# Second block of a two-block decoder: attention and output projection placed between the units of the input projection

## The chip, the cores and the metric
The kernel runs on one core of one Trainium2 chip. The metric is the device time of one execution in microseconds (us), from the first to the last instruction and what the launch puts around them. TensorE (PE) multiplies matrices into PSUM; VectorE (DVE) and ScalarE (ACT) compute on PSUM and SBUF; GpSimd (POOL) does the same slowly and issues transfers of its own; SyncE (SP) issues the loads of the weights. Each engine takes its instructions in program order, and they wait for one another through semaphores.

## The reference, cut to what matters
Two blocks of two layers each run one after the other on 256 tokens of width 1024. The change is nearly all in the second block:

```
for l in range(2):
    mod = cond @ w_mod[l] + b_mod[l]                 # six vectors of 1024
    h = rms_norm(x, norm_mix) * (1 + sc_a) + sh_a
    mq, mk, mv, dq, dk, dv = split(h @ w_in)         # six times 512 columns
    # q and k: rms_norm over each head of 64 (times a weight of 64), then a rotation of the
    # first 16 elements by cos, sin of the position
    o_m = rms_norm(causal_attention(mq, mk, mv))     # 8 heads of 64
    o_d = rms_norm((softmax(s1) - lam * softmax(s2)) @ dv) * (1 - lam_init)   # 4 heads, v of 128
    x = x + g_a * (concat(o_m, o_d) @ w_out)
    h = rms_norm(x, norm_ffn) * (1 + sc_f) + sh_f
    x = x + g_f * ((silu(h @ w_gate) * (h @ w_up)) @ w_down)
```

With 256 tokens and a block of 256, the "moba" attention is a plain causal one.

## The kernel before
All weights come through a ring of six slots of 1 MB each (`ring`), filled by SP in the order in which PE uses them. A layer of the second block has these parts, one after the other:

- **Modulation.** POOL has formed `w_mod * cond` for this layer beforehand (`modulation(l)`, 24 pieces of 1 MB, into `pmod`). PE sums it over partitions (L1385, L1390).
- **Input projection.** Twelve units of 256 columns (L882, 32 matmul records each), into four PSUM banks in turn. After each of the eight units of q and k, ACT squares (L802), DVE sums per head (L1929), ACT takes the root with `Sqrt` (L804), DVE takes the reciprocal (L1932), scales (L1935), multiplies by the norm's weight (L1937) and rotates (twelve instructions of 128x32, L1943 to L1948). PE transposes the result (L1143) behind the next unit, and ACT copies it to `qT` (L807). The four units of v are only copied (L797).
- A barrier of all engines.
- **Attention** in eight units: four pairs of moba heads, four diff heads. For each, PE forms scores (L1053), DVE scales and masks (L1570) and takes row maxima (L1574, L1579), ACT takes four exponentials with row sums (L616), DVE divides (L1587 to L1597), PE transposes the probabilities (L1094), ACT copies them (L631), PE multiplies with v (L1114), and DVE copies the result to `om` (L1609). At the end the outputs are squared, summed, rooted (L813) and scaled on DVE and ACT, in two halves (L1614 to L1630).
- A barrier, 16 transposes of `om` (L849), four copies (L818), and the **output projection** (L1033, 64 records, first all of token tile 0, then all of tile 1).
- **Residual and norm**: DVE multiplies by the gate and adds (L1956, L1958), ACT sums squares (L768) and takes a root (L771), DVE scales (L1881), PE transposes (L849), DVE modulates (L1890). Then the gated feed-forward (L875, L893).

For layer 1, POOL's `modulation(1)` starts after layer 0's second barrier of the second block, that is, after the attention:

```
                if b == 2 * BARRIERS_1 + 1:
                    modulation(1)
```

The tables of the rotation are computed by DVE and ACT (`Sin`) at the start of the second block.

Of the kernel before, what the change touches and what calls it, by code (L numbers as in the profile page):

```python
# [14 lines left out]
P = 128  # L15
D = 1024
# [36 lines left out]
          ("gate_b", 32), ("norm_mix", 8), ("norm_ffn", 8), ("b_mod", 48)]  # L53
N_PAR = sum(n for _, n in PARAMS)
N_PARAM_LOADS = DEPTH * (len(PARAMS) + 5) + 4
GAINS = [("moba_q", 64), ("moba_k", 64), ("diff_q", 64), ("diff_k", 64), ("moba_out", 64), ("diff_sub", 128),
         ("lambda", 256)]
# [57 lines left out]
def build(nc, a, out, known):  # L115
    with ExitStack() as ctx:
# [31 lines left out]
        small = sb("small", [P, 256])  # L148
        ARENA = 27700
# [5 lines left out]
        def view(*shape, parts=P, at=None):  # L155
# [7 lines left out]
            names = "abcd"[:len(shape)]  # L163
# [82 lines left out]
        top[0] = 3000  # L246
        gains = view(sum(n for _, n in GAINS))
        grow = view(2, D)
        modT, Amod = view(32), view(2, KT)
        cosb, sinb = view(NT, ROPE_HALF), view(NT, ROPE_HALF)  # L250
        ang = view(4, NT * ROPE_HALF)
        vtm, om = view(NT, D), view(NT, D)
        tok_scaled = vtm
        qT = view(16, SEQ)
        ys_tmp = view(NT, D, at=top[0])
        tq, tsq = view(2, 512), view(2, 512)
        rope = view(6, NT * 4 * ROPE_HALF)
        angi = ang[:, 3, :].bitcast(I32)
        Sm2, PT2 = view(4, 2, PACK), view(2, 2, PACK)
# [4 lines left out]
        ys_tmp = tok_scaled  # L264
        oT8 = oT[:, 0:8, :]

        def units_of(seg):
            return UNITS1 if seg == "b1" else UNITS2

        def o_bank(seg, i):  # L270
            return 6 if seg == "b1" else 6 + i % 2
# [12 lines left out]
        goff = {}  # L284
        o = 0
        for name, n in GAINS:
            goff[name] = (o, n)
            o += n

        def prm(l, name, i=0, n=1):  # L290
            return par[:, l, poff[name][0] + i:poff[name][0] + i + n]

        def gain(name):
            return gains[:, goff[name][0]:goff[name][0] + goff[name][1]]
# [11 lines left out]
        def unit_list(segment):  # L306
# [21 lines left out]
            elif kind == "in2":  # L328
                w = kview(a["w_in_2"][l])
                for i in range(12):  # L330
                    yield ("in2", l, i), [(0, 256, w[:, :, UNIT * i:UNIT * i + 256])]
# [99 lines left out]
        def _(pool):  # L431
            barrier = barrier_of(pool)

            def step(ins):
                ins.then_inc(*made("pool"))
                pool.wait_ge(S.sem("pool"), S.count["pool"])
# [74 lines left out]

            for kind in CREDITED:
                if known:
                    pool.sem_inc(S.sem(kind), known.per_turn[kind])
            for b in range(N_BARRIERS):
# [9 lines left out]
                if b == 2 * BARRIERS_1 + 1:  # L525
                    modulation(1)

        @block.scalar
        def _(act):
            barrier = barrier_of(act)  # L530

            def step(ins, *key):
                ins.then_inc(*made("act", *key))

# [66 lines left out]
            def norm_roots(*key):  # L601
                for t in range(NT):
# [3 lines left out]
            def attention(l, units, Sb, PTb, seg):  # L606
                n = len(units)
                for i in range(n + 2):
                    if i < n:
                        u, b = units[i], i % 2  # L610

                        act.wait_ge(*ready("dve", "nm", seg, l, u))
                        for qt, (k0, nk) in enumerate(KEYS):
                            for h in range(2):
                                s = Sb[:, i % 4, h, k0:k0 + nk]
                                step(act.activation(s, s, ACT.Exp, bias=nm[:, b, qt, h:h + 1],  # L616
                                                    accum_out=den[:, b, qt, h:h + 1]), "exp", seg, l, u)
                        if u[0] == "swa":
                            step(act.activation(es[:, b], es[:, b], ACT.Exp), "exp", seg, l, u)
                    if seg == "b1" and i in G[7]:  # L620
                        gates(l, 1, (7,))
                    if i >= 2:
                        turned(units[i - 2], l, seg, i - 2, PTb)

            def turned(v, l, seg, i, PTb):

                act.wait_ge(*ready("pe_job", "pt", seg, l, v))
# [1387 lines left out]
```

## Time and profile before

| what | value |
|---|---|
| median of 3 runs | 2629.13 us (2629.05 to 2632.51) |
| span of the profiled execution | 2622.4 us |
| what lies around the span, against the median | 6.7 us |
| PE busy | 2340.6 us, 89% of the span |
| layer 1, second block, input projection | 2197.8 to 2287.2 |
| layer 1, attention up to the second barrier | 2287.2 to 2339.7 |
| layer 1, turning `om`, output projection | to 2373.8 |

The profiled execution has no time of its own beside its span; the span stands 6.7 us under the median of the other runs. The granted clock of PE is given in the windows as a share of full speed (1.00 is 2.4 GHz, 0.50 is 1.2 GHz).

### The profile page before, as it was taken

The numbers are of one execution on the slowest core, as the hardware profiler recorded it, in microseconds if no ns is written. First come the engines' busy times: TensorE is split into PE (matmuls) and PEld (weight loads), VectorE is DVE, ScalarE is ACT, GpSimd is POOL, SyncE is SP. The second block draws the span as 40 slices with busy tenths as digits, with TensorE's granted clock in tenths as the row PEclk, the third lists the DMA queues.
The fourth block names the chain that finished last, engine by engine and source line by source line (L and its number), as shares of the span: only waits on it lengthen the run. The fifth ranks groups of instructions, "written<-read, shape, count | busy, mean of one in ns | idle before, by whom it ended". The sixth has DMA issues, their size and how long they took to land.

```text
span 2622.4 us, 29759 instructions
## 1 busy us (share of the span) xinstructions
PE 2340.6 (89%) x12542; PEld 1827.3 (70%) x12542; DVE 700.0 (27%) x1477; ACT 334.9 (13%) x756; POOL 451.1 (17%) x328
## 2 busy tenths in 40 slices
PE   8997788999899958939899999979589998968998
PEld 7786565777687846637788888868457777746776
DVE  0132643000204163471211111154620104451011
ACT  0031220000002123000000000021300001230000
POOL 2000000000000000399910000000199930000000
PEclk9999789999999977969999999979689998969999
DMA  8332212444533221269978888644167744403443
GB/s 248 113 97 81 88 57 97 130 151 130 183 109 113 97 89 41 67 220 329 347 264 265 264 266 265 227 150 145 64 208 236 268 155 134 144 1 115 147 148 103
DMA packets 313420, 416.61 MB, mean 159 GB/s; under 512 B 15356, under 2 KB 272616, under 8 KB 313320
## 3 DMA queue, kind: packets, MB, share of 16 engines
q1 hardware_dynamic: 290112, 346.64, 40.5%
q0 software_dynamic: 13056, 50.33, 5.7%
q10 hardware_dynamic: 10152, 18.20, 2.0%
q8 instruction: 75, 1.23, 0.2%
q14 instruction: 25, 0.20, 0.0%
HBM read 414.10 MB, written 1.05 MB: 158 GB/s over the span
## 4 chain that ended last, share of the span: by engine, by line
PE 50%; DVE 7%; DMA 2%; ACT 1%; issue 0%; SPq 0%; DVEq 0%; ACTq 0%
PE psum L875 22%; PE psum L882 6%; PE psum L893 6%; PE psum L978 5%; PE psum L1033 3%; DMA ring<-in_exp_w 2%; PE psum L1363 1%; PE psum L938 1%; PE psum L1385 1%; PE psum L1018 1%; DVE small L1574 1%; DVE xT L1890 1%; DVE arena L1570 0%; PE psum L1390 0%; DVE arena L1514 0%
## 5 line engine op out<-in xcount | busy, mean ns | idle before, releaser
L875 PE MATMUL psum<-xT,ring 128*128 128x256 f32 (+1 forms) x3904 | 874.5, 385 | 15.0 <-DVE xT L1890 5.5
L875 PEld LDWEIGHTS psum<-xT,ring 128*128 128x128 f32 (+1 forms) x3904 | 742.4, 191 | 148.5 <-issue 23.7
L875 PEld LDWEIGHTS psum<-arena,ring 128*128 128x128 f32 x2816 | 320.0, 192 | 28.7 <-issue 23.8
L875 PE MATMUL psum<-arena,ring 128*128 128x128 f32 x2816 | 322.4, 276 | 11.0 <-DMA ring<-in_exp_w 8.8
L893 PE MATMUL psum<-ring,arena 128*128 128x512 f32 x528 | 231.5, 592 | 0.0
L882 PE MATMUL psum<-ring,xT 128*128 128x256 f32 (+3 forms) x1024 | 213.5, 368 | 6.4 <-DVE xT L1890 6.4
L882 PEld LDWEIGHTS psum<-ring,xT 128*128 128x128 f32 x1024 | 186.2, 200 | 29.1 <-DVE xT L1890 6.9
L519 POOL IOTA arena<- 128x128 int32 x1 | 0.2, 234 | 1061.4 <-DVEq L371 1061.4
L1474 DVE TENSOR_TENSOR arena<-arena,psum 128x512 f32<-128x512 f32 (+1 forms) x36 | 23.2, 643 | 594.2 <-PE psum L875 594.2
L893 PEld LDWEIGHTS psum<-ring,arena 128*128 128x128 f32 x528 | 100.4, 190 | 113.4 <-issue 111.8
L504 POOL TENSOR_TENSOR arena<-arena,cond 128x2048 f32<-128x2048 f32 x48 | 173.4, 3613 | 7.6 <-DMA arena<-in_w_mod 6.7
L978 PE MATMUL psum<-ring,arena 128*128 128x512 f32 x352 | 157.8, 593 | 1.5 <-DVE arena L1551 1.5
L491 POOL DMA_DIRECT2D arena<-in_w_mod x48 | 44.3, 923 | 583.1 <-DVEq L371 569.8
L1551 DVE TENSOR_TENSOR arena<-arena,psum 128x256 f32<-128x256 f32 (+1 forms) x48 | 19.1, 399 | 360.0 <-PE psum L875 359.6
L507 POOL TENSOR_TENSOR arena<-arena 128x1024 f32<-128x1024 f32 x48 | 113.7, 2369 | 3.8
L978 PEld LDWEIGHTS psum<-ring,arena 128*128 128x128 f32 x352 | 63.9, 191 | 66.7 <-issue 65.0
L560 ACT ACTIVATE arena<-psum 128x512 f32<-128x512 f32 (+1 forms) x36 | 20.2, 561 | 639.4 <-PE psum L875 639.4
L1094 PE MATMUL psum<-ident,arena 128*128 128x128 f32 x168 | 38.2, 385 | 46.4 <-DVE arena L1597 18.7
L1363 PE MATMUL psum<-oT,arena 128*128 128x256 f32 x320 | 71.3, 386 | 5.4 <-DMA arena<-in_w_branch 5.4
L1363 PEld LDWEIGHTS psum<-oT,arena 128*128 128x128 f32 x320 | 61.9, 194 | 14.8 <-DMA arena<-in_w_branch 6.2
L616 ACT ACTIVATE arena<-arena,small 128x256 f32<-128x256 f32 (+1 forms) x128 | 56.6, 442 | 112.0 <-DVE small L1579 111.9
L1094 PEld LDWEIGHTS psum<-ident,arena 128*128 128x128 f32 x168 | 28.0, 199 | 61.4 <-DVE arena L1597 23.8
(352 smaller groups left out, 1977.9 us busy)
## 6 DMA issues: line engine op xcount, KB each, us to landing
ring<-in_exp_w SPq DMA_DIRECT2D x120, 1024.0 KB, 7.9
ring<-in_w_in SPq DMA_DIRECT2D x80, 1024.0 KB, 5.1
arena<-in_w_mod POOLq DMA_DIRECT2D x48, 1024.0 KB, 8.3
ring<-in_ffn_w SPq DMA_DIRECT2D x30, 1024.0 KB, 5.9
ring<-in_w_gate SPq DMA_DIRECT2D x20, 1024.0 KB, 7.6
ring<-in_w_up SPq DMA_DIRECT2D x20, 1024.0 KB, 10.0
ring<-in_w_down SPq DMA_DIRECT2D x20, 1024.0 KB, 5.0
ring<-in_w_out SPq DMA_DIRECT2D x16, 1024.0 KB, 4.8
```

The source lines that it names most:

```text
L491: pool.dma_start(modw[:, j % 3, :].rearrange("p (k c) -> p k c", k=KT), w_mod[:, :, j * UNIT:(j + 1) * UNIT]).then_inc(S.sem("modw%d" % (j ...
L504: step(pool.tensor_tensor(w.rearrange("p (k c) -> p k c", k=KT), w.rearrange("p (k c) -> p k c", k=KT), cond[:].unsqueeze(2).broadcast_to( ...
L507: step(pool.tensor_tensor(w[:, 0:1024], w[:, 0:1024], w[:, 1024:2048], ALU.add))
L616: step(act.activation(s, s, ACT.Exp, bias=nm[:, b, qt, h:h + 1], accum_out=den[:, b, qt, h:h + 1]), "exp", seg, l, u)
L875: ins = pe.matmul(dst, w[:, k * 256 + c0:k * 256 + c0 + m], act_t[:, k, :], start=(k == 0), stop=(k == KT - 1))
L882: ins = pe.matmul(dst, act_t[:, k, t * P:t * P + P], w[:, k * 256 + c0:k * 256 + c0 + n], start=(k == 0), stop=(k == KT - 1))
L893: ins = pe.matmul(psum[:, 4 + 2 * t + h, :], gT[:, s % 3, f * 256 + t * P:f * 256 + t * P + P], w2[:, f * D + h * 512:f * D + h * 512 + 51 ...
L938: ins = pe.matmul(psum[:, 6 + k // 4, (k % 4) * P:(k % 4) * P + P], x[:, t, k * P:k * P + P], gather[:, t, :], start=(t == 0), stop=(t == ...
L978: ins = pe.matmul(psum[:, 4 + h, :], gT[:, s % 3, f * P:f * P + P], w2[:, f * D + h * 512:f * D + h * 512 + 512], start=(s == 0 and f == 0 ...
L1033: ins = pe.matmul(psum[:, 4 + 2 * t + h, :], src[:, k, t * P:t * P + P], ws[k2][:, i * D + h * 512:i * D + h * 512 + 512], start=(k == 0), ...
L1094: ins = pe.transpose(psum[:, 4 + h, o:o + P], Sb[:, i % 4, h, o:o + P], ident[:])
L1363: ins = pe.matmul(dst, (wb_first[:, k] if k < 5 else wb_last[:, k - 5])[:, c * P:c * P + P], oT[:, k, :], start=(k == rows_of[0]), stop=(k ...
```

## The change
The attention, the norm of its outputs and the output projection of the second block are written in one order with the twelve projection units, by hand, for PE, ACT and DVE. The two barriers are gone. In detail:

- The units come in the order `ORDER2`; the projection uses two banks instead of four.
- The head norm: the root is taken as `Exp(-0.5 * Ln(...))` on ACT instead of `Sqrt` and a reciprocal on DVE; the norm's weight is multiplied in by ACT's copy to `qT` (`keep_heads`) and, for the first 16 elements, is held in the rotation's tables (`tabA`, `tabB`), which POOL builds (`turn_tables`). The rotation takes seven instructions instead of twelve.
- The probabilities of the moba heads are not divided: the norm of the output makes up for it, with the square of the row sum times eps added to the sum of squares (`out_sums`). For the diff heads only the second half is scaled, by `lam` times the ratio of the row sums (`differ`).
- The norm of the outputs runs for each unit (`square_outs`, `out_sums`, `out_roots` with Ln and Exp, `norm_outs`, `keep_outs`), on PSUM, and each unit's output is transposed by itself (`turn_outs`).
- The output projection is cut into 16 pieces (`join(l, t, k)`), put between the last units.
- `modulation(1)` waits for the last output projection piece of layer 0. The angles and `Sin` move to before the first block's feed-forward. `norm_roots` makes a first `Sqrt` before it waits. Twelve small loads of parameters are added at the start, seven per layer leave ACT's queue, and five per layer enter POOL's.

The core of the diff (kept: what ACT does per unit, one stretch of each engine's order, and the place of `modulation(1)`):

```diff
-                        step(act.activation(tsq[:, n, :], psum[:, i % 4, :], ACT.Square), "sq", l, i)
-                        act.wait_ge(*ready("dve", "headsum", l, i))
-                        step(act.activation(rt16[:, 8 * n:8 * n + 8], ss16[:, 8 * n:8 * n + 8], ACT.Sqrt,
-                                            bias=eps[:, 2:3], scale=1.0 / HD), "headroot", l, i)
+            def head_roots(l, n):
+                i = ORDER2[n]
+                b = QK.index(i) % 2
+                act.wait_ge(*ready("dve", "headsum", l, i))
+                step(act.activation(ri8[:, b], ss8[:, b], ACT.Ln, bias=eps[:, 2:3]), "headlog", l, i)
+                act.wait_ge(*ready("act", "headlog", l, i))
+                step(act.activation(ri8[:, b], ri8[:, b], ACT.Exp, scale=-0.5), "headroot", l, i)
+            def out_roots(l, p):
+                m, d = (4, HD) if p < 4 else (2, P)
+                act.wait_ge(*ready("dve", "outsum", l, p))
+                step(act.activation(ro4[:, p % 2, 0:m], os4[:, p % 2, 0:m], ACT.Ln, scale=1.0 / d), "outlog", l, p)
+                act.wait_ge(*ready("act", "outlog", l, p))
+                step(act.activation(ro4[:, p % 2, 0:m], ro4[:, p % 2, 0:m], ACT.Exp, scale=-0.5), "outroot", l, p)
...
+            def turn_outs(l, p):
+                pe.wait_ge(*ready("dve", "om", l, p))
+                pe.wait_ge(*ready("act", *turned_last[0]))
...
-                barrier()
-                attention(l, "b2", Sm2, PT2)
-                barrier()
-                turn(om, ("o2", l), None)
-                pe.wait_ge(*ready("act", "xt", "o2", l, 3))
-                out_rows("out2", l, oT8)
+                project(l, 7)
+                turn_heads(l, 6)
+                turn_outs(l, 0)
+                weigh2(l, 1)
+                turn_probs2(l, 2)
+                scores2(l, 3)
+                project(l, 8)
...
+                exp2(l, 2)
+                square_heads(l, 7)
+                head_roots(l, 7)
+                keep_heads(l, 6)
+                keep_outs(l, 0)
...
-                if b == 2 * BARRIERS_1 + 1:
+                if b == 2 * BARRIERS_1 - 1:
+
+                    pool.wait_ge(*ready("pe_job", "out2", 0, NT - 1))
                     modulation(1)
+                    turn_tables(1)
```

How it moves instructions, at two places. **PE, input projection of a layer.** Before, a row of L882 is a unit and L1143 the turning of a q or k unit; nothing else stands there until the twelfth unit:

```order
L1143 MATMUL psum<-ident,arena 128x128 x4
L882 MATMUL psum<-ring,xT 128x256 x16
L1143 MATMUL psum<-ident,arena 128x128 x4
L882 MATMUL psum<-ring,xT 128x256 x48
L1143 MATMUL psum<-ident,arena 128x128 x4
```

In the changed kernel, around `project(l, 7)` and `project(l, 8)` (L1038 is a unit, L1292 `turn_heads`, L1302 `turn_outs`, L1341 `weigh2`, L1327 `turn_probs2`, L1316 `scores2`):

```order
L1038 MATMUL psum<-ring,xT 128x256 x16
L1292 MATMUL psum<-ident,arena 128x128 x4
L1302 MATMUL psum<-ident,arena 128x128 x2
L1341 MATMUL psum<-arena 128x64 x6
L1327 MATMUL psum<-ident,arena 128x128 x6
L1316 MATMUL psum<-arena 128x128
L1316 MATMUL psum<-arena 128x256
L1316 MATMUL psum<-arena 128x128
L1316 MATMUL psum<-arena 128x256
L1038 MATMUL psum<-ring,xT 128x256 x16
```

The turning of an output and three small attention steps have moved in between two units, and each has waits of its own.

**ACT, the same stretch.** Before, a head's part is square, root, copy, with no table load after the first (L802, L804, L807):

```order
L802 ACTIVATE arena<-psum 128x512
L804 ACTIVATE small<-small,eps 128x8
L807 COPY arena<-psum 128x512
L802 ACTIVATE arena<-psum 128x512
L804 ACTIVATE small<-small,eps 128x8
```

In the changed kernel, from `square_heads(l, 7)` to the exponentials of unit 3 (L831 square, L838 and L840 `head_roots`, L847 `keep_heads`, L897 `keep_outs`, L883 `square_outs`, L876 `keep_probs`, L890 and L892 `out_roots`):

```order
L831 ACTIVATE arena<-psum 128x512
L838 ACT_TABLE_LOAD
L838 ACTIVATE small<-small,eps 128x8
L840 ACT_TABLE_LOAD
L840 ACTIVATE small<-small 128x8
L847 ACTIVATE arena<-psum,par 128x512
L897 ACTIVATE oT<-psum,par 128x256
L883 ACTIVATE arena<-psum 128x256
L876 COPY arena<-psum 128x768
L890 ACT_TABLE_LOAD
L890 ACTIVATE small<-small 128x4
L892 ACT_TABLE_LOAD
```

Each pair of Ln and Exp has brought a table load of its own ahead of each of the two; there are 16 such pairs in a layer.

## Rows read from the trace of the kernel before

**Rows 1.** Windows: bounds, length, busy us (records) of PE, PEld, DVE, ACT, POOL, clock, DMA.
```profile
1923.20:1939.50 16.30, 3.68 (x16) 3.28 (x16) 14.24 (x16) 2.73 (x4) 15.55 (x8) 0.64 0.73 254
...
2197.80:2287.20 89.40, 88.67 (x416) 76.58 (x416) 40.46 (x138) 14.91 (x30) 0.00 (x0) 0.98 0.39 130
2287.20:2342.20 55.00, 30.41 (x184) 25.29 (x185) 43.76 (x87) 22.36 (x76) 0.00 (x0) 0.68 0.06 20
...
2373.80:2383.90 10.10, 3.40 (x17) 2.60 (x17) 8.31 (x16) 2.73 (x4) 0.00 (x0) 0.73 0.37 136
```

**Rows 2.** The chain that ended last, both layers' projection: start, us, what.
```profile
1746.62 15.77 PE psum L882 x64
...
2197.85 15.56 PE psum L882 x64
2213.41 0.51 PE psum L1143 x4
2213.93 6.91 PE psum L882 x32
```

**Rows 3.** Timeline of PE, layer 1's attention at full clock: start, us, operation, idle before.
```profile
2310.83 0.85 PE L1094 MATMUL psum<-ident,arena 128*128 128x128 f32 x6 [1.67 <-DVE arena L1570]
2311.52 1.45 PE L1114 MATMUL psum<-arena 128*128 128x64 f32 x12
2312.90 0.93 PE L1053 MATMUL psum<-arena 64*128 64x128 f32 x8
2314.81 0.52 PE L1094 MATMUL psum<-ident,arena 128*128 128x128 f32 x3 [0.99 <-ACT arena L631]
```

**Rows 4.** Timeline, PE in the output projection of layer 1.
```profile
2344.32 29.38 PE L1033 MATMUL psum<-ring,oT 128*128 128x512 f32 x64 [0.92 <-ACT oT L818]
```

**Rows 5.** Timeline of ACT and DVE, one head unit of layer 1.
```profile
2206.55 0.60 ACT L802 ACTIVATE arena<-psum 128x512 f32<-128x512 f32 x1 [4.71 <-PE psum L882]
2207.16 1.28 ACT L804 ACT_TABLE_LOAD   x1
2208.45 0.30 ACT L804 ACTIVATE small<-small,eps 128x8 f32<-128x8 f32 x1
2209.09 0.69 DVE L1935 TENSOR_TENSOR arena<-psum,small 128x512 f32<-128x512 f32 x1
2213.02 0.19 DVE L1948 TENSOR_TENSOR arena<-arena 128x32 f32<-128x32 f32 x1
```

**Rows 6.** Timeline of ACT, first block: loads for Ln (behind an Exp), then for Exp.
```profile
264.71 1.28 ACT L740 ACT_TABLE_LOAD   x1
...
280.45 1.28 ACT L616 ACT_TABLE_LOAD   x1
```

**Rows 7.** Timeline, attention of layer 1: exponentials, copy, masking, maxima.
```profile
2297.48 0.40 ACT L616 ACTIVATE arena<-arena,small 128x128 f32<-128x128 f32 x1 [1.87 <-DVE small L1579]
...
2299.25 0.77 ACT L631 COPY arena<-psum 128x768 f32<-128x768 f32 x1
...
2305.78 0.96 DVE L1570 SCALAR_TENSOR_TENSOR arena<-psum,mask 128x768 f32<-128x768 f32 x1 [3.54 <-PE psum L1053]
2306.77 1.14 DVE L1574 TENSOR_REDUCE small<-arena 128x2 f32<-128x256 f32 x2
```

**Rows 8.** Timeline, DVE's add to x in layer 0 and in layer 1.
```profile
1923.92 4.49 DVE L1958 TENSOR_TENSOR x<-x,arena 128x512 f32<-128x512 f32 x1
...
2374.53 0.69 DVE L1958 TENSOR_TENSOR x<-x,arena 128x512 f32<-128x512 f32 x1
```

**Rows 9.** Timeline of POOL, layer 0: `modulation(1)`, its start and its last instruction; PE at its use.
```profile
1889.32 2.67 POOL L491 DMA_DIRECT2D arena<-in_w_mod  x3 [569.83 <-DVEq L371]
1895.31 3.60 POOL L504 TENSOR_TENSOR arena<-arena,cond 128x2048 f32<-128x2048 f32 x1 [3.32 <-DMA arena<-in_w_mod]
2120.14 0.72 POOL L509 TENSOR_TENSOR arena<-arena 128x256 f32<-128x256 f32 x1
2174.09 13.81 PE L1385 MATMUL psum<-ones,arena 128*128 128x1 f32 x64 [4.20 <-DVEq L371]
```

More of the change, by code:

```diff
@@ L601, in norm_roots @@
             def norm_roots(*key):
+                step(act.activation(warm[:], eps[:, 0:1], ACT.Sqrt), "warm", *key)
+                act.wait_ge(*ready("act", "warm", *key))
                 for t in range(NT):
@@ L608, in attention @@
+            def attention(l):
+                n = len(UNITS1)
                 for i in range(n + 2):
                     if i < n:
[L610 to L617, printed above, removed]
@@ L618, in attention @@
[L618 to L620 removed]
+                        exps(l, i, UNITS1[i])
+                    if i in G[7]:
                         gates(l, 1, (7,))
                     if i >= 2:
[L623 to L627 removed]
+                        turned(l, i - 2)
@@ L757, in _ @@
                     step(act.activation(e2, e2, ACT.Exp), "router_exp")
+                if l == 0:
+                    act.wait_ge(*ready("dve", "angles"))
+                    for side, sign in ((0, -1.0), (1, 1.0)):
+                        step(act.activation(trig_sin[:, :, side, :], two(ang[:, 1, :]), ACT.Sin, scale=sign))
+                    step(act.activation(trig_cos[:], two(ang[:, 2, :]), ACT.Sin), "trig")
                 ffn("ffn1" if l == 0 else "moe", l)
@@ new lines, in _ @@
+                turn_probs2(l, 2)
+                scores2(l, 3)
+                project(l, 8)
+                turn_heads(l, 7)
+                turn_outs(l, 1)
+                weigh2(l, 2)
+                turn_probs2(l, 3)
+                project(l, 9)
+                turn_outs(l, 2)
+                weigh2(l, 3)
+                scores2(l, 4)
+                project(l, 10)
+                turn_heads(l, 9)
+                turn_probs2(l, 4)
+                turn_outs(l, 3)
+                scores2(l, 5)
@@ new lines, in _ @@
+                project(l, 11)
+                turn_heads(l, 10)
+                weigh2(l, 4)
+                turn_probs2(l, 5)
+                join(l, 0, 0)
+                join(l, 0, 1)
+                scores2(l, 6)
+                turn_outs(l, 4)
+                weigh2(l, 5)
+                join(l, 0, 2)
+                join(l, 0, 3)
+                scores2(l, 7)
+                turn_probs2(l, 6)
+                turn_outs(l, 5)
+                join(l, 0, 4)
+                join(l, 0, 5)
@@ new lines, in _ @@
+                join(l, 1, 0)
+                turn_probs2(l, 7)
+                weigh2(l, 6)
+                join(l, 1, 1)
+                join(l, 1, 2)
+                turn_outs(l, 6)
+                weigh2(l, 7)
+                join(l, 1, 3)
+                join(l, 1, 4)
+                join(l, 0, 6)
+                turn_outs(l, 7)
+                join(l, 1, 5)
+                join(l, 1, 6)
+                join(l, 0, 7)
+                join(l, 1, 7)
+                turn(xs, ("ffn", l), ("xs", "ffn", l))
@@ L1841, in _ @@
                     step(dve.memset(turn_no, 0.0))
+                if l == 0:
+                    angles()
                 ffn("ffn1" if l == 0 else "moe", l)
```

777 lines of the change are left out of this document (504 added, 273 removed).

## The prediction
> **What bounds the kernel now.** I read the windows by stage first. In the input projection of the second block PE is busy 88.67 of 89.40 us; in the attention behind it 30.41 of 55.00, at a mean clock of 0.68, while DVE is busy 43.76 [rows 1]. So the projection is bound by PE, the attention by a chain through DVE and ACT, and the output projection by PE again (64 records in 29.38 us) [rows 4]. The chain of waits says the same: one projection unit of 32 records takes 6.91 us, and the turning of a head unit 0.51 between two [rows 2]. I call "the stage" what lies between the first projection record and the first DVE instruction after the output projection: 1923.20 - 1746.62 = 176.6 us in layer 0 and 2373.80 - 2197.85 = 175.95 us in layer 1 [rows 1, 2]. Only there, and in the residual behind it, can much move.
>
> **PE's work in the new stage.** At full clock, by spacing of starts where rows give it:
> - 12 units x 6.91 = 82.9; 8 `turn_heads` x 0.51 = 4.1 [rows 2].
> - 8 `turn_probs2`: six transposes take 2311.52 - 2310.83 = 0.69 until the next start, three about half, 0.36: 4 x 0.69 + 4 x 0.36 = 4.2. Moba `weigh2`: 2312.90 - 2311.52 = 1.38, say 1.42; diff `weigh2` with half the records, 128 wide, estimated at 0.85: together 9.1. `scores2`: busy 0.93, less the 0.16 by which the transposes' busy time exceeds their spacing, 0.77 x 8 = 6.2. `turn_outs`, two transposes, about 0.29 x 8 = 2.3 [rows 3].
> - 16 `join` with 4 records of 512 columns each, twice a projection record's 6.91 / 32 = 0.216: 64 x 0.43 = 27.5 [rows 2]; today's 29.38 has a slow start in it [rows 4].
>
> The sum is 136.3 us. If nothing else stood in the way, 40 us a layer would go. The question is what stands in the way.
>
> **ACT's work, and table loads.** The root of a head unit was 0.60 (square) and 0.30 (`Sqrt`) on ACT, with one load of 1.28 for all eight units [rows 5]. Now each root is Ln and Exp, and the order of ACT shows a load ahead of each. That is what the trace of the first block shows too: the Ln behind an Exp pays a load (264.71), and the Exp behind that Ln pays one again (280.45) [rows 6]. With starts 1.29 to 1.30 apart [rows 5], 32 loads are 41.6 us of ACT per layer. The rest of ACT in the stage: 8 squares x 0.60, 8 x (0.31 + 0.20), 8 copies of heads x 0.57, 4 of v x 0.5, 8 times four exponentials (1.87 each, from 2297.48 to 2299.25 plus the hand-over), copies 4 x 0.70 and 4 x 0.38 (half the columns of the 0.77), 8 output squares x 0.30, roots 8 x 0.45, output copies x 0.36 [rows 5, 7]: about 43.5. So ACT has 85 us of work beside PE's 136: it doesn't bound by its sum, but it takes its steps in order and PE waits for single ones.
>
> The Trainium skill (ScalarE: Activation LUTs, Table sets: the hidden batching unit) has Ln and Exp in one set, so that a pair costs one load; by that nearly all 32 would vanish. Our rows and the order speak against it.
>
> **Where PE stands.** I laid the three queues beside each other in program order: a step starts when its engine is free and what it waits for is done; hand-overs 0.06 to 0.1 us. On DVE: head sum 0.69, scaling 0.69, six small products at 0.19 and a closing add of 0.30 [rows 5]; `masked` 0.98, then 1.35 until the maxima are out; `differ` 1.3 [rows 7]. Time runs from the stage's start. PE then stands at eight places:
> - 64.8, `turn_outs(0)`: **5.5 us**. It wants PSUM bank 2, which ACT empties with `keep_heads(6)`. In ACT's order four exponentials (64.0 to 65.8) and `square_heads(7)`, `head_roots(7)` stand before it: 65.8 + 0.60 + 1.30 + 0.31 + 1.30 + 0.20 = 69.5, the copy till 70.1, and PE goes on at 70.3. Behind PE's wait stand `weigh2(1)`, `turn_probs2(2)`, `scores2(3)` and projection unit 8.
> - 44.2, `turn_probs2(0)`: 1.9, for the exponentials, which wait for the first `masked`, behind `heads(4)` on DVE.
> - 111.9, `turn_probs2(5)`: 2.0, for `differ(5)`. 124.8, `turn_outs(5)`: 1.8, for the output norm of unit 5, that is two loads.
> - 80.8, 101.4, 123.9, 137.0: 1.0, 1.2, 0.6, 0.8.
>
> Sum 14.8. The first unit after DVE's modulation runs slowly: 15.56 - 6.91 = 8.65 instead of 6.91, so 1.7 [rows 2]; and I take another 1.7 for a fallen clock after the stand of 5.5. **New stage: 136.3 + 14.8 + 3.4 = 154.5.** With the loads at nothing the same layout gives 141.4 before the clock's part.
>
> **The residual behind it.** `join` finishes token tile 0 only 1.72 us before tile 1, where it was 13 us. DVE's four steps for tile 0 (4 x 0.72) are then no longer hidden, and tile 1 starts 2.9 - 1.7 = 1.2 later: +1.2 per layer. In layer 0 the window behind the output projection is 16.30 us against 10.10 in layer 1, because POOL works beside it (15.55 busy), and an add of x takes 4.49 instead of 0.69 [rows 1, 8]. `modulation(1)` now starts when the last `join` is done, and its first product came 6 us after its first fetch [rows 9]: the adds are over by then. -6.2.
>
> **What costs nothing, and its cover.** POOL's `modulation(1)` takes 2120.86 - 1889.32 = 231.5 us; it must be in before L1385 of layer 1, which stands 2174.09 - 1923.20 = 250.9 after the output projection [rows 1, 9]: 19 us to spare, of which the five transfers and twelve small products of `turn_tables` are no part, since DVE needs those only 24 us later. The angles go beside the first 10 us of the first feed-forward. The weights' ring keeps its order; the four slots of the output weights are given back 1.7 to 13 us before the end, as before within a few us. Moving the angles away gains nothing, since PE's L1385 ran beside them. The early `Sqrt` of `norm_roots` gains nothing either: the load it moves lay before the first token tile's root, beside matmuls.
>
> **Sum.** Layer 0: 154.5 - 176.6 = -22.1, +1.2, -6.2. Layer 1: 154.5 - 175.95 = -21.4, +1.2. Together -47.3 on the span of 2622.4, which gives 2575.1; the median lies 6.7 above the span, so **2582 us**, 1.8% faster.
>
> **Rivals.**
> 1. *The loads hide or fall away.* A stage of 141.4 + 1.7 = 143.1: 2629.1 - 33.5 - 32.85 + 2.4 - 6.2 = 2559. For it: at other places loads ran before the wait was over. Against it: the 5.5 us stand begins with ACT busy, not waiting. Chance 0.08.
> 2. *The small steps cost more.* 44 small steps and 16 joins now stand between units, each with two semaphores to wait for; 0.2 us more each, or some stands twice as long, is 13 us a layer: 2608. For it: in the attention PE stood 1.67 and 0.99 us at such places [rows 3]. Chance 0.16.
> 3. *A load costs about twice what its row says, and the stage comes out slower.* At 2.66 us per change of set ACT has 129 us beside PE's 136, and the same layout gives a stage of 179.2 + 3.4 = 182.6: +6.0, +6.65, +2.4, -6.2 = 2638. Even is reached at a stage of 178, that is about 2.5 us a load. Against it: a load begins 0.01 after the activation before it and the next activation 1.29 after its start [rows 5]. The Trainium skill (ScalarE: Activation LUTs, What ACT_TABLE_LOAD costs) gives 1283 ns and a drain of 1380 ns, 2.66 us in all, which is this rival; the 1283 agrees with the rows, the drain isn't seen in them. Chance 0.05.
> 4. *PE's clock doesn't come back.* The attention ran at 0.68 with PE busy for 30.41 of 55.00 [rows 1]. If from 112 us on, where stands of 2.0, 0.6, 1.8 and 0.8 follow one another, PE ran at 1.2 GHz, its 34 us of work would take 34 more and swallow the 5 of stands: +29 a layer, 2640. Against it: PE would be busy nine tenths there. Chance 0.04.
> 5. Mine, 2568 to 2600: 0.67.
>
> **Range.** Mine reaches to 2600; with most of rival 2 it is 2568 to 2606, which holds 0.8. A change of 0.2% is about what a measurement of this kernel can tell from none. Faster by more than that 0.92, same 0.03 (between rivals 2 and 3), slower 0.05.
>
> **What the profile of the changed kernel would show.** A stage of 150 to 160 us in both layers, with PE busy over 0.85 of it. 32 loads per layer on ACT, 1.28 each. PE's longest wait at the transposes of the first output, some 5 us, released by ACT. A residual window of layer 0 like that of layer 1, near 11 us. L1385's counterpart in layer 1 not waiting for POOL. I would be wrong if loads stood with gaps around them, if PE's windows showed 0.50 in the stage's last third, or if PE waited for POOL.

## The result, and the profile after

The changed kernel takes **2582.03 us** (median of 4 runs, 2578.82 to 2583.52) against 2629.09 us for the kernel before (4 runs, 2628.10 to 2632.51): a ratio of 0.9816, with a 95% interval of 0.9804 to 0.9827. It is 47 us, 1.8%, faster. The profiled execution has a span of 2581.8 us and a time of 2583.52 us, so 1.7 us lie around the span. Of the runs below, one of `e_before_pool` took 4422.67 us at a mean clock of 0.746 and is left out of every comparison.

In the page's first part PE is now busy for 91% of a shorter span, with nearly the same busy time in all as before (less in the stage, more in the first block, see below):

```profile
PE 2338.6 (91%) x12542; PEld 1822.6 (71%) x12542; DVE 632.3 (24%) x1351; ACT 430.3 (17%) x888; POOL 462.8 (18%) x368
```

The windows of the changed kernel: stage and residual of layer 0, then of layer 1 (bounds, length, busy us and records of PE, PEld, DVE, ACT, POOL, clock, DMA share, GB/s). They answer to [rows 1]:

```profile
1756.90:1909.10 152.20, 141.77 (x668) 109.06 (x668) 54.93 (x165) 85.74 (x173) 0.00 (x0) 0.97 0.32 104
1909.10:1920.50 11.40, 3.69 (x17) 3.27 (x17) 9.45 (x18) 5.46 (x8) 5.44 (x4) 0.70 0.92 308
2178.00:2332.50 154.50, 144.03 (x668) 109.72 (x668) 54.97 (x165) 85.86 (x173) 0.00 (x0) 0.96 0.31 103
2332.50:2343.80 11.30, 3.68 (x16) 3.27 (x16) 9.40 (x18) 5.45 (x8) 0.00 (x0) 0.70 0.27 93
```

The stage was 176.6 and 175.95 us before [rows 1, 2]. It is now 152.2 and 154.5, with PE busy for 93% of it. The window behind it went from 16.30 to 11.40 in layer 0 and from 10.10 to 11.4 in layer 1 (the last row is cut a little early; by the records it is 2332.43 to 2343.84) [rows 1]. Together: -24.4 - 21.5 - 4.9 + 1.3 = -49.5 us.

The stage of layer 0 in the kernel before, as one window:

```profile
1746.62:1923.20 176.58, 149.88 (x668) 115.50 (x668) 87.59 (x230) 40.77 (x113) 29.01 (x17) 0.87 0.35 116
```

So of the 24.4 us in layer 0 some 8 are PE's own time, the same 668 records at a granted clock of 0.97 instead of 0.87 (141.77 instead of 149.88 us), and 16 are time in which PE stood (26.7 before, 10.4 now).

Where PE still stands in layer 1: its timeline (start, us, instruction, and in brackets the idle time before it and what the profile names as the releaser). All seven waits of the stage sum to 10.3 us; these are the stretch around the longest, and three shorter ones:

```profile
2243.62 0.60 PE L1292 MATMUL psum<-ident,arena 128*128 128x128 f32 x4
2248.57 0.41 PE L1302 MATMUL psum<-ident,arena 128*128 128x128 f32 x2 [4.35 <-DVE arena L1927]
...
2253.71 8.41 PE L1038 MATMUL psum<-ring,xT 128*128 128x256 f32 x32
2263.48 0.41 PE L1302 MATMUL psum<-ident,arena 128*128 128x128 f32 x2 [0.92 <-ACT arena L847]
...
2294.29 0.55 PE L1327 MATMUL psum<-ident,arena 128*128 128x128 f32 x3 [1.22 <-DVE arena L1970]
...
2306.84 0.44 PE L1302 MATMUL psum<-ident,arena 128*128 128x128 f32 x2 [1.71 <-DVE arena L1992]
```

ACT in the same stretch (same columns):

```profile
2244.05 0.18 ACT L867 ACTIVATION_READ_ACCUMULATOR arena<-arena,small 128x1 f32 x1
2244.14 0.57 ACT L831 ACTIVATE arena<-psum 128x512 f32<-128x512 f32 x1
2244.73 1.28 ACT L838 ACT_TABLE_LOAD   x1
2246.03 0.30 ACT L838 ACTIVATE small<-small,eps 128x8 f32<-128x8 f32 x1
2246.34 1.28 ACT L840 ACT_TABLE_LOAD   x1
2247.64 0.21 ACT L840 ACTIVATE small<-small 128x8 f32<-128x8 f32 x1
2247.75 0.67 ACT L847 ACTIVATE arena<-psum,par 128x512 f32<-128x512 f32 x1
```

`turn_outs(0)` (L1302) was ready to go at 2248.57 - 4.35 = 2244.22. It wants the bank that `keep_heads(6)` (L847) empties, and ACT comes to that copy at 2247.75, after a square and a head root with its two table loads. The profile names DVE's L1927 as the releaser, but the copy on ACT is what ends just before PE goes on; `e_swap` below decides it.

ACT's groups in layer 1's stage show the loads, 32 in a layer (line, operation, count, busy us, mean ns, idle before):

```profile
L838 ACT ACT_TABLE_LOAD x8 | 10.3, 1283 | 0.1
L840 ACT ACT_TABLE_LOAD x8 | 10.3, 1283 | 0.1
L890 ACT ACT_TABLE_LOAD x8 | 10.3, 1283 | 0.1
L892 ACT ACT_TABLE_LOAD x8 | 10.3, 1283 | 0.1
```

### The profile page after: what moved, and what is told of

Its sections match the earlier page's. It is cut to its first block, busy times and chain, and to the rows that moved or that the text cites. A ratio compares the mean times of both kernels' runs of the same rounds, so it can differ in the third digit from the quotient of the medians.

```text
span 2581.8 us, 29817 instructions
## 1 busy us (share of the span) xinstructions
PE 2338.6 (91%) x12542; PEld 1822.6 (71%) x12542; DVE 632.3 (24%) x1351; ACT 430.3 (17%) x888; POOL 462.8 (18%) x368
## 4 chain that ended last, share of the span: by engine, by line
PE 49%; DVE 6%; ACT 3%; DMA 2%; issue 1%; SPq 0%; ACTq 0%; DVEq 0%
PE psum L1031 23%; PE psum L1049 6%; PE psum L1134 6%; PE psum L1038 5%; PE psum L1358 2%; PE psum L1586 1%; PE psum L1094 1%; DMA ring<-in_exp_w 1%; PE psum L1189 1%; PE psum L1608 1%; PE psum L1174 1%; ACT arena L867 1%; DVE xT L2212 1%; PE psum L1341 0%; PE psum L1613 0%
## 5 line engine op out<-in xcount | busy, mean ns | idle before, releaser
L1038 PE MATMUL psum<-ring,xT 128*128 128x256 f32 (+3 forms) x1024 | 217.1, 372 | 6.4 <-DVE xT L2212 6.4
L1038 PEld LDWEIGHTS psum<-ring,xT 128*128 128x128 f32 x1024 | 187.5, 201 | 33.9 <-DVE xT L2212 6.9
L610 ACT ACTIVATE arena<-psum 128x256 f32<-128x256 f32 (+1 forms) x48 | 17.6, 366 | 369.8 <-PE psum L1031 369.8
L631 ACT ACTIVATE arena<-psum,par 128x256 f32<-128x256 f32 x64 | 26.9, 471 | 249.5 <-PE psum L1031 249.5
L508 POOL TENSOR_TENSOR arena<-arena 128x512 f32<-128x512 f32 x48 | 63.2, 1317 | 3.8
```

What stands on the lines that cost most here:

```text
L508: step(pool.tensor_tensor(w[:, 0:512], w[:, 0:512], w[:, 512:1024], ALU.add))
L631: step(act.activation(zb[:, b, c, :], psum[:, banks[j % len(banks)], i * 256:i * 256 + 256], ACT.Identity, bias=prm(l, "gate_b", b * KT + ...
L1038: ins = pe.matmul(dst, act_t[:, k, t * P:t * P + P], w[:, k * 256 + c0:k * 256 + c0 + n], start=(k == 0), stop=(k == KT - 1))
```

## The experiments

Ratios are always to the kernel before, run on the same chip beside the experiment. "Projection to feed-forward" is the time from a layer's first projection record to its first feed-forward record, that is the stage and the residual together: 192.9 and 186.0 us in the profile of the kernel before, 163.6 and 165.8 in that of the changed kernel.

### c_after: the changed kernel once more

No edit.

> The changed kernel once more, beside the three below, on the same chip. Both theories: 2582 us (2579 to 2585). Its profile tells how far the profiled execution differs from the one shown: the second block should repeat within 2 us, the first block may not.

Measured: 2578.10 us (2577.91 to 2583.32), ratio 0.9812 (0.9798 to 0.9825). Projection to feed-forward was 166.8 and 165.8. So layer 0 is not always the quicker one: its stage took 155.39 us here and 152.2 in the first profile, with PE busy 144.98 and 141.77. The waits are the same to 0.01 us; the difference is PE's time, that is its clock.

### e_noload: no table loads in the stage

```diff
-                step(act.activation(ri8[:, b], ss8[:, b], ACT.Ln, bias=eps[:, 2:3]), "headlog", l, i)
+                step(act.activation(ri8[:, b], ss8[:, b], ACT.Square, bias=eps[:, 2:3]), "headlog", l, i)
```

The same is done in `out_roots`. This kernel leaves the logarithm out, so its roots are not roots.

> Ln is replaced by Square in the 32 roots of the second block, which leaves out the logarithm (the roots are other numbers); every step, wait and copy stays, and the 64 table loads are gone. Theory (the loads stand on the path, by the layout of the three queues): the stage falls to 141 + 1.7 for the slow first unit, from 152 and 154 us, the wait before the first output's transposes falls from 4.5 to about 2, and the kernel to 2561 us (2556 to 2566). Rival (the loads hide behind PE, what is left of the waits comes from the many small steps): no more than 4 us, 2578 or above.

Measured: 2563.38 us (2556.53 to 2567.75), ratio 0.9745 (0.9729 to 0.9761). No load is left in the stage. Layer 1's stage and residual in its windows:

```profile
2166.97:2312.30 145.33, 141.49 (x668) 109.22 (x668) 54.71 (x165) 44.76 (x141) 0.00 (x0) 0.97 0.34 109
2312.30:2323.70 11.40, 3.39 (x17) 3.15 (x17) 9.46 (x18) 5.46 (x8) 0.00 (x0) 0.85 0.24 92
```

ACT's busy time fell by 41.1 us a layer, from 85.86 to 44.76, and the stage by 9.1. The waits sum to 3.7 instead of 10.3 us, and the longest, still at `turn_outs(0)`, is 2.21. PE in the 10 us behind that wait:

```profile
2234.25:2244.25 10.00, 10.00 (x45) 8.29 (x46) 4.28 (x16) 3.82 (x13) 0.00 (x0) 0.66 0.18 72
```

So even a stand of 2.21 us was followed by a fallen clock, which costs more here (10.00 us at 0.66, some 3.4) than the stand did. The pair of Ln and Exp therefore costs some 15 us in the whole kernel, about a fifth of the 82 us that its loads take on ACT.

### e_moreload: one more load in each root

```diff
                 step(act.activation(ri8[:, b], ss8[:, b], ACT.Ln, bias=eps[:, 2:3]), "headlog", l, i)
+                step(act.activation(warm[:], eps[:, 0:1], ACT.Sqrt), "w2", l, i)
```

The same is done in `out_roots`. That makes 48 loads in a layer.

> Between each Ln and its Exp stands a Sqrt of one column that nobody reads, so that a pair has three loads and 0.2 us more instead of two: 24 us of ScalarE per layer more. Theory (ScalarE's steps are on the path): the layout gives +14.4 us per layer, 2611 us (2604 to 2618), the wait before the first output's transposes about 8.5 us. Rival (ScalarE has 85 us of work beside 136 of TensorE, so there is room): under +8 us in all, below 2590.

Measured: 2615.43 us (2610.38 to 2618.79), ratio 0.9946 (0.9932 to 0.9959). Layer 1's stage in its windows, and PE's longest wait in its timeline:

```profile
2191.24:2363.35 172.11, 150.77 (x668) 113.61 (x668) 54.80 (x165) 109.45 (x205) 0.00 (x0) 0.90 0.29 92
```

```profile
2269.07 0.66 PE L1304 MATMUL psum<-ident,arena 128*128 128x128 f32 x2 [8.38 <-DVE arena L1929]
```

Read with `e_noload`: ACT's work goes 44.8, 85.9, 109.5 us and the stage 145.3, 154.5, 172.1. The first 41 us on ACT cost 9, the next 24 cost 18 (14.4 were forecast). The waits go 3.7, 10.3, 21.3; the rest of the growth is PE's busy time, 141.5, 144.0, 150.8, which is the same 668 records at a lower granted clock (0.97, 0.96, 0.90).

### e_sqrt: one root on ACT, the reciprocal back on DVE

```diff
-                step(act.activation(ri8[:, b], ss8[:, b], ACT.Ln, bias=eps[:, 2:3]), "headlog", l, i)
-                act.wait_ge(*ready("act", "headlog", l, i))
-                step(act.activation(ri8[:, b], ri8[:, b], ACT.Exp, scale=-0.5), "headroot", l, i)
+                step(act.activation(ri8[:, b], ss8[:, b], ACT.Sqrt, bias=eps[:, 2:3]), "headroot", l, i)
...
                 dve.wait_ge(*ready("act", "headroot", l, i))
+                step(dve.reciprocal(ri8[:, b], ri8[:, b]))
```

The same is done for the outputs' roots. 15 loads are left in a layer, where `Sqrt` and `Exp` change places.

> The roots as the kernel before had them, Sqrt on ScalarE and a reciprocal on VectorE, in the changed kernel's order: the order shows 15 loads in a layer's stage instead of 32, since Sqrt changes the set only where exponentials lie between. Theory: stage 142.4 + 1.7, 9 us per layer less, 2564 us (2558 to 2570), with the first output's wait near 2.5 us. Rival (the form of the root doesn't matter, the interleaving sets the time): 2580 us or above; VectorE's extra 3.5 us per layer would make it no faster.

Measured: 2564.50 us (2561.82 to 2569.63), ratio 0.9755 (0.9742 to 0.9769). Projection to feed-forward was 158.3 and 158.2, the waits sum to 5.0, the longest is 2.53. Its time can't be told from that of the kernel with no loads at all (2561.82 to 2569.63 against 2556.53 to 2567.75): with 15 loads they are nearly all hidden, and DVE's 16 reciprocals a layer (0.17 to 0.20 us each) cost nothing visible. Behind the wait of 2.53 the clock is at 0.66 for 10 us, as in `e_noload`.

### e_swap: `keep_heads(6)` ahead of unit 7's root

```diff
                 exp2(l, 2)
+                keep_heads(l, 6)
                 square_heads(l, 7)
                 head_roots(l, 7)
-                keep_heads(l, 6)
```

> One step moved in ScalarE's order: keep_heads(6), which empties the bank that the first output's transposes want, stands before square_heads(7) and head_roots(7) instead of behind them. Theory: the longest wait, 4.4 us in both layers, falls to under 1.5, some of it comes back at the next output (1.0 to 1.6), and the clock keeps its level there: 3 to 4.5 us a layer, 2572 to 2574 beside 2578 to 2582 of the changed kernel. Rival (TensorE waits there for VectorE's normed output, which the profile names as releaser): no change in that wait.

Measured: 2566.67 us (2563.03 to 2570.17), ratio 0.9767 (0.9754 to 0.9780). All 32 loads are still there. PE's timeline at the same place:

```profile
2236.74 0.60 PE L1292 MATMUL psum<-ident,arena 128*128 128x128 f32 x4
2238.20 0.41 PE L1302 MATMUL psum<-ident,arena 128*128 128x128 f32 x2 [0.87 <-ACT arena L847]
```

The wait is 0.87 instead of 4.35, and now the profile names ACT's copy as the releaser. So it was the copy on ACT that PE waited for. The waits of a layer fell by 3.5 us, but projection to feed-forward fell to 157.6 in both layers, that is by 6.0 and 8.3 (by 9.2 and 8.2 against `c_after`). I had expected only 3 to 4.5. The rest is the clock, in windows of the changed kernel (layer 1: the stand, the 10 us behind it, and 5 us behind the wait of 1.71 further on):

```profile
2238.00:2248.50 10.50, 6.22 (x31) 5.25 (x29) 5.87 (x18) 9.57 (x19) 0.00 (x0) 1.00 0.28 105
2248.50:2258.50 10.00, 9.93 (x44) 8.26 (x45) 4.35 (x16) 6.50 (x15) 0.00 (x0) 0.66 0.01 2
...
2306.80:2311.80 5.00, 4.96 (x9) 2.18 (x10) 2.87 (x8) 2.33 (x9) 0.00 (x0) 0.66 0.00 0
```

and of `e_swap` (the place of the stand, 10 us behind the same wait of 1.71, and its whole stage):

```profile
2240.00:2250.00 10.00, 9.08 (x51) 7.50 (x49) 4.89 (x16) 8.99 (x20) 0.00 (x0) 1.00 0.17 59
2293.20:2303.20 10.00, 9.97 (x31) 4.82 (x31) 3.80 (x11) 6.10 (x15) 0.00 (x0) 1.00 0.09 8
2170.97:2317.13 146.16, 139.24 (x668) 106.75 (x668) 54.82 (x165) 85.62 (x173) 0.00 (x0) 0.99 0.34 108
```

After the stand PE is busy all the time, but at 0.66 of full speed, between its levels of 1.2 and 2.4 GHz. Without the stand the clock stays at 2.4 GHz, and the same 668 records take 139.24 instead of 144.03 us. Of these 4.8 us, 3.4 lie behind the stand (9.93 us at 0.66). The rest lies behind the wait of 1.71 (4.96 us at 0.66), and that wait is still there in `e_swap`, unchanged, with the clock at 1.00. In the changed kernel the clock fell behind it in layer 1 and, in `c_after`, in both layers, but not in layer 0 of the first profile. So the fall at the second place isn't shown to come from the stand that the edit removed; what decides there stays open.

### e_before_pool: the kernel before, with `modulation(1)` behind the output projection

```diff
                 if b == 2 * BARRIERS_1 + 1:
+                    pool.wait_ge(*ready("pe_job", "out2", 0, NT - 1))
                     modulation(1)
```

> The kernel before with one wait added: modulation(1) of GpSimd starts when the output projection of layer 0 is done, as in the changed kernel. Theory (GpSimd's work lengthens VectorE's adds of x): the residual window of layer 0 falls from 16.3 to 10 or 11 us and nothing else moves, 2623 us (2620 to 2626); GpSimd still finishes 15 to 20 us before its sum is wanted. Rival (the adds are long for another reason, the transfers for instance): 2629.

Measured: 2625.18 us over the 11 runs that are compared (2620.54 to 2629.12), 2626.02 over all 12, ratio 0.9993 (0.9984 to 1.0002). That is inside the theory's 2620 to 2626, but the kernel before takes 2627.34 on this chip: the whole time doesn't tell it from no change, and the interval ends at 4.2 us less, short of the 6 less that the theory gives. The place itself does. Its timeline, DVE and POOL behind layer 0's output projection:

```profile
1927.39 0.69 DVE L1959 TENSOR_TENSOR x<-x,arena 128x512 f32<-128x512 f32 x1
1928.84 0.69 DVE L1959 TENSOR_TENSOR x<-x,arena 128x512 f32<-128x512 f32 x1
1935.45 3.60 POOL L504 TENSOR_TENSOR arena<-arena,cond 128x2048 f32<-128x2048 f32 x1 [5.64 <-DMA arena<-in_w_mod]
```

The adds to x take 0.69 instead of 4.49 (the first; the second took 1.99) [rows 8]. The window behind the output projection, from the end of its last record, is 10.51 us (1926.56 to 1937.07); by the same count it was 16.43 (1923.09 to 1939.52), and 16.30 from DVE's first instruction [rows 1]. The edit moves `modulation(1)`'s transfers too, so the rival has to be read in this window:

```profile
1926.56:1937.07 10.51, 3.07 (x17) 2.44 (x17) 8.30 (x16) 2.73 (x4) 4.29 (x4) 0.75 1.02 346
```

The DMA engines are busy all the time there (share 1.02, 346 GB/s, against 0.73 and 254 in the kernel before), and the adds are short all the same: it is not the transfers. Projection to feed-forward fell by 5.4, from 192.9 to 187.5, in layer 0, and rose by 0.9 in layer 1, where nothing was edited. The second block as a whole took 898.5 us, against 900.2 and 902.0 in the two profiles of the kernel before. GpSimd finished 12.0 us before its sum was wanted (2159.46 to 2171.44), not 15 to 20. The Trainium skill (SBUF — State Buffer, Who interferes with whom) says that a DVE instruction with two SBUF inputs contends with a GpSimd instruction that reads SBUF, and that this contention is an exclusive lock; the 4.49 beside POOL's product of 3.61 us and the 0.69 without it agree.

### e_serial: all the new steps, in the old order

The steps of the changed kernel on all three engines are put back into "first all twelve units, then all eight attention units, then all of the output projection", without barriers. ACT's new order, for example, behind the projection:

```diff
+                exp2(l, 3)
+                keep_probs(l, 2)
+                square_outs(l, 1)
+                out_roots(l, 1)
+                keep_outs(l, 0)
```

> The changed kernel's 180 steps per layer, all of them, in another order on the three engines: first the twelve projection units with their heads, then the attention units one behind the other, then the output projection by token tiles. No barrier comes back. Theory (the gain is the interleaving; the steps themselves are no cheaper with 32 table loads): the layout gives a stage of about 190 + 3.4 us, longer than the 176 of the kernel before, and a kernel of about 2655 us (2640 to 2670). Rival (the gain is the missing barriers, the seven rotation steps instead of twelve and the missing divisions): 2600 us or below.

Measured: 2661.43 us (2661.37 to 2661.89), ratio 1.0130 (1.0116 to 1.0145): 34 us slower than the kernel before, 83 slower than the changed one. The stage is 197.0 and 196.3 us, where 193.4 was forecast. The projection and most of the attention of layer 1 in its windows:

```profile
2214.66:2302.00 87.34, 87.34 (x412) 76.72 (x413) 23.29 (x82) 35.42 (x51) 0.00 (x0) 0.98 0.40 133
2302.00:2376.00 74.00, 36.28 (x187) 29.50 (x186) 28.63 (x76) 46.10 (x115) 0.00 (x0) 0.60 0.05 15
```

and one turn of its chain in the timeline:

```profile
2333.18 1.28 ACT L890 ACT_TABLE_LOAD   x1
2334.70 1.28 ACT L892 ACT_TABLE_LOAD   x1
2336.23 0.42 DVE L1992 TENSOR_TENSOR arena<-psum,small 128x256 f32<-128x256 f32 x1 [2.28 <-ACT small L892]
2336.57 0.94 DVE L1954 SCALAR_TENSOR_TENSOR arena<-psum,mask 128x768 f32<-128x768 f32 x1
2340.06 0.90 PE L1327 MATMUL psum<-ident,arena 128*128 128x128 f32 x3 [7.08 <-DVE arena L1970]
```

The masking of a later unit (L1954) stands on DVE behind the norm of an output (L1992), which waits for two loads. That unit's exponentials wait for the masking, and so does `differ` (L1970) of the unit before it, which stands behind it on DVE and for which PE's transposes (L1327) wait 7.08 us. DVE's busy time in attention is down (28.63 in these 74 us, against 43.76 in 55.00 [rows 1]), and it doesn't help. Of the new steps by themselves, in this order, nothing is gained; against it, the changed kernel gains 83 us by giving PE projection units and output pieces to do meanwhile. The order inside the attention was one of several possible ones, and all 32 loads a layer are in it, some on this chain. No run has the old order with `Sqrt` and 15 loads, so it isn't shown that seven rotation steps and no barriers would gain nothing there.

### e_join: token tile 0 finished one piece earlier

```diff
-                join(l, 1, 6)
                 join(l, 0, 7)
+                join(l, 1, 6)
                 join(l, 1, 7)
```

> One edit on the changed kernel: join(0, 7) before join(1, 6) instead of behind it, so that token tile 0 is done 3.4 us before tile 1 instead of 1.7. Theory (VectorE's four adds for tile 0 weren't hidden): from the end of the last join to the first feed-forward matmul 10.1 us instead of 11.4 in both layers, and the stage itself unchanged. Rival (that window is set by the norm behind the adds alone): 11.4 again. The time can't tell 2.5 us; the window can.

Measured once: 2580.47 us. Its windows behind the last piece, layer 0 and 1:

```profile
1906.03:1916.32 10.29, 3.68 (x17) 3.27 (x17) 8.31 (x16) 4.96 (x8) 3.84 (x4) 0.62 0.90 304
2329.40:2339.69 10.29, 3.68 (x17) 3.26 (x16) 8.32 (x16) 4.96 (x8) 0.00 (x0) 0.61 0.28 102
```

10.29 instead of 11.40 in both layers. The swap takes back 1.1 of the 1.3 us that the pieces' order had cost.

### e_best: the three together

`e_sqrt`, `e_swap` and `e_join` in one kernel.

> Three edits on the changed kernel: Sqrt and reciprocal for the roots (15 loads a layer instead of 32), keep_heads(6) ahead of square_heads(7), and the last piece of token tile 0 one place earlier, before join(1, 6). Theory: the layout gives a stage of 140.7 + 1.7 for the slow first unit, 142 to 143 us, and a window behind it of 10 us instead of 11.4: 2556 us (2550 to 2561), no wait of TensorE over 1.2 us in the stage. Rival (the two edits on ScalarE buy the same wait, so that the second adds nothing to e_sqrt): 2562 to 2565.

Measured: **2555.91 us** (2552.58 to 2558.13), ratio 0.9721 (0.9708 to 0.9734), 22 to 26 us faster than the change as it was made (2578.10 and 2582.03). Layer 1's stage in its windows, and its longest wait in the timeline:

```profile
2162.33:2304.39 142.06, 138.70 (x668) 106.80 (x668) 58.91 (x182) 61.40 (x141) 0.00 (x0) 0.99 0.34 111
```

```profile
2240.06 0.41 PE L1298 MATMUL psum<-ident,arena 128*128 128x128 f32 x2 [0.92 <-ACT arena L845]
```

PE is busy for 138.70 of 142.06 us. Little is left to win in the stage by moving steps.

### c_before: the kernel before once more

No edit.

> The kernel before once more, for its profile. The profile that the prediction read had a span 6.7 us under the median, and the prediction took that for what lies around a span. If the profiled execution was instead a quick one of its kind, this span is within 2 us of its own time, about 2627, with the second block's windows as before (within 1 us) and the difference in the first block. If 6.7 us lie around every span of this kernel, the span is 2622 again beside a time of 2629.

Measured once: 2633.72 us at a span of 2632.0, so 1.7 around the span here too. From projection to feed-forward it is the same as the first profile to 0.2 us (192.94 and 186.16), and the second block as a whole is 1.7 longer (902.0 against 900.2), but it begins at 1730.0 us instead of 1722.2. The window from 320 us up to the second block, in `before` (its first profile), then in `c_before`:

```profile
320.00:1722.20 1402.20, 1256.08 (x7283) 983.85 (x7282) 346.62 (x645) 164.02 (x335) 218.05 (x124) 0.93 0.53 174
320.00:1730.03 1410.03, 1266.01 (x7299) 989.82 (x7297) 347.47 (x648) 165.23 (x341) 218.05 (x124) 0.93 0.53 173
```

The same stretch in the first profile of the changed kernel, and in `c_after`:

```profile
320.00:1731.83 1411.83, 1267.64 (x7302) 992.01 (x7300) 354.27 (x681) 168.57 (x352) 224.63 (x147) 0.93 0.53 173
320.00:1723.50 1403.50, 1259.93 (x7293) 987.37 (x7293) 351.36 (x675) 166.93 (x346) 224.66 (x147) 0.93 0.53 174
```

Both kernels have executions in which the second block begins near 1723 and near 1731 us, and the others lie between. It isn't the chip alone: `e_serial` and `c_before` ran on the same one and begin it at 1724.3 and 1730.0. In these rows PE's busy time is 9.9 and 7.7 us longer, for nearly as many records, where the stretch is 7.8 and 8.3 longer: it is PE's own time, which goes with the clock.

## Why the prediction was right, and where not

The forecast was 2582.0 us, and 2582.03 was measured. The mechanism is the one forecast, but that the number came out to a tenth is luck: terms that were off by 1 to 5 us cancelled, and the medians shown above lie 47.1 us apart where those of `c_after` lie 50.4 apart.

**What bounds, and where the gain comes from: right.** PE's work fills the stage. `e_serial` shows that the same steps without the placing are slower than the kernel before, so the gain needs the placing. Of the stage's gain 8.1 of 24.4 us in layer 0 and 5.6 of 21.5 in layer 1 are PE's own time at a higher clock. The forecast had that in it, since it priced all of PE's work at full clock, but didn't say so.

**The stage: 154.5 forecast, 152.2 to 155.4 measured, out of three terms that were each off.**
- PE's work with the slow first unit was 136.3 + 1.7 = 138.0. `e_swap`, where the clock stays up, has 139.24 (layer 1): 1.2 more.
- The stands were 14.8 and came to 10.3, in seven places instead of eight. The longest was 5.5 and came to 4.35: ACT began the square behind its four exponentials 0.08 us before PE arrived (2244.14 and 2244.22), not 1.0 after. ACT's stretch from there to the copy's end was 4.3 in the working and 4.28 in the trace.
- The fallen clock was 1.7, a bare assumption, and at one place. Against `e_swap` it is 144.03 - 139.24 = 4.8 in layer 1, some 3.4 behind the longest stand and the rest behind a wait of 1.71. In layer 0 it is 2.5, all behind the stand, and 5.7 in `c_after`, at both places.

So +1.2, -4.5 and +3.1 in layer 1 nearly cancel. The step that failed is the one that took the fallen clock as a small extra of fixed size at one place: 1.7 us forecast, 2.5 to 5.7 measured. It made me expect too little of `e_swap`, and in `e_moreload` it is again a good part of the loss.

**The table loads: right.** The forecast went by the order and [rows 5, 6]: 32 loads a layer at 1.28 us, each with the next activation 1.29 us after its start. The trace has these 32, at 1.28 us, with the next activation 1.30 after. The Trainium skill (ScalarE: Activation LUTs, Table sets: the hidden batching unit) would have one load for a pair of Ln and Exp; here each of the two brought its own, and `e_noload` measures what they cost in all, 15 us. The layout without loads said 143.1 for the stage; 143.8 and 145.3 were measured. Rival 1, that the loads hide by themselves, is refuted by those 15 us. Rival 3, a load at 2.66 us, is refuted by the starts on ACT and by `e_moreload`, which with half as many loads again is still faster than the kernel before.

**Many small steps (rival 2): not seen.** Small steps between units follow one another with no gap in PE's timeline, outside the seven waits, and PE's time for all 668 records is only 1.2 us over the sum of its parts (`e_swap`). **Rival 4, a clock that doesn't come back: half seen.** It fell behind the stand at 64.8, where I hadn't placed it, and was back at full speed 10 us later. It also fell where I had placed it, in the stage's last third, behind the wait for `turn_outs(5)`: 0.66 over 5 us in layer 1 and in `c_after`'s layer 0. The prediction named that as a sign of being wrong; it cost some 1.7 us there and not 29, since it came back each time. In `e_serial`, with PE busy half the time, it did stay low (0.60 over 74 us).

**The residual: right.** +1.2 was forecast for token tile 0 being late, 1.3 was measured in layer 1 (10.10 to 11.40), and `e_join` takes 1.1 of it back. For POOL's work beside the adds -6.2 was forecast. `e_before_pool` shows -5.9 in the window; in the changed kernel 16.30 became 11.40, that is -4.9, or -6.2 beside the tile's +1.3. What this is worth in the whole time of `e_before_pool` stays open: its 11 runs are 2 us below the kernel before, with an interval (-4.2 to +0.5) that holds zero and not the 6 forecast, and the profile shows 0.9 us of it lost again in layer 1.

**POOL: right in kind, the margin was less.** POOL's timeline of the changed kernel, and PE at the use of the result:

```profile
2141.10 0.72 POOL L509 TENSOR_TENSOR arena<-arena 128x256 f32<-128x256 f32 x1
...
2154.11 6.13 PE L1608 MATMUL psum<-ones,arena 128*128 128x1 f32 x28 [4.20 <-DVEq L371]
```

`modulation(1)` was ready 12.3 us before its use and not 19. I had reckoned the time until the use from the kernel before, 250.9 us, whose residual was 5 us longer by the very collision that I took away; it is 245.0 now. The first product also came 8.1 us after the first fetch and not 6, which changed nothing.

**The span and what lies around it: wrong.** I took 6.7 us between the span and the median. Each profiled execution with a time of its own has 1.7. The other 5 were the difference between one execution and the others: `c_before` has a second block 1.7 us longer and a first block 7.8 us longer than the first profile. My sum of -47.3, set on the median, was what gave 2582. In the two first profiles the second block (from its modulation on) shrank by 50.2, from 900.2 to 850.0, and the first block grew by 9.6, which the comparison of `c_after` (1723.5) with `c_before` (1730.0) has the other way round. The second block of those two shrank by 49.1 (902.0 to 852.9), so the change in it is 49 to 50 us where 47.3 was forecast. I can't assign those first-block differences to the change.

**What costs nothing.** The early `Sqrt` and the earlier angles were taken as worth nothing. No run tests them, and the profiles can't tell: the nine with these changes reach the second block at 1723.5 to 1731.8 us, the three without at 1722.2 to 1730.0. That they are worth nothing isn't shown; an effect of several us is not seen.

## What to carry to other kernels

Price a stand of PE with the slow stretch behind it: the 3.5 us of waiting that `e_swap` took away brought 6 to 9 us a layer, and in layer 1 the clock fell as much behind 2.21 us (`e_noload`) as behind 4.35. When steps are placed by hand into another engine's gaps, put the copy that empties a bank ahead of anything with a table load in it, and keep one table function where a cheap instruction on an idle engine can do the rest: here 16 reciprocals on DVE did away with 17 loads of 32 in a layer. And set a change's sum on a median, never on one span, since an execution's own difference can be as large as a term.

## What the runs showed of the hardware

- The granted clock can cost as much as the wait before it, or more: 4.35 us of standing, then 10 us at 0.66 with PE busy 9.93 of them (some 3.4 us lost); 2.21 us of standing in `e_noload`, then the same 0.66 over 10 us (both in layer 1). Behind a wait of 1.71 it fell in some executions (0.66 over 5 us) and stayed at 1.00 in others.
- Ln and Exp in turn brought a table load of 1.28 us each, 32 in a layer for 16 pairs. All 64 together took 82 us of ACT and cost the kernel 15; 16 more a layer cost it 37.
- One kernel's executions differ by PE's clock. In layer 0 the same waits gave 141.77 us of PE time in one and 144.98 in another: 0.73 instead of 0.57 over the 10 us behind the stand, and no fall at the second place instead of 0.66 over 5 us. The first block took 1722 to 1732 us in either kernel, with a clock of 0.50 in two profiles, 0.61 in `c_after` and 0.67 in the first profile of the kernel before over the same 20 us (300 to 320).
- The releaser that the profile names for a wait of two semaphores can be the wrong one (L1927 for L847, 4.35 us), as an edit of one line showed.
